# Block heads of a Strassen-Winograd feed-forward kernel: operand sums made from the residual rows through two PSUM banks

## The reference

```python
def rms_norm(x, g):
    xf = x.astype(F32)
    y = xf * lax.rsqrt(jnp.mean(xf * xf, axis=-1, keepdims=True) + EPS)
    return (y * g.astype(F32)).astype(x.dtype)

def swiglu(x, w_in, w_out):
    gate, up = jnp.split(x @ w_in, 2, axis=-1)
    return (jax.nn.silu(gate) * up) @ w_out
...
for l in range(DEPTH):
    x = x + 0.5 * swiglu(rms_norm(x, norm_g[l, 0]), ffn_w_in[l, 0], ffn_w_out[l, 0])
    h = rms_norm(x, norm_g[l, 1])
    ...
    x = x + y
    x = x + 0.5 * swiglu(rms_norm(x, norm_g[l, 2]), ffn_w_in[l, 1], ffn_w_out[l, 1])
```

## Time and profile before

| what | value |
|---|---|
| median of 3 runs | 2114.4 us (2114.19, 2114.4, 2116.44) |
| profiled execution, its own time | 2116.01 us |
| its span, first to last instruction | 2114.2 us |
| TensorE busy | 2052.2 us, 97% |
| VectorE busy | 1257.2 us, 59% |
| ScalarE busy | 872.1 us, 41% |
| GpSimd busy | 1301.0 us, 62% |
| mean granted TensorE clock | 0.991 |
| DMA | 190.61 MB, mean 90 GB/s |

### The profile page before, as it was taken

One profiled execution on the slowest core, in us unless ns is written; L12 is line 12 of the kernel. 1 busy time (PEld: TensorE's weight loads), 2 busy tenths in 40 slices (PEclk: granted clock), 3 DMA queues, 4 the chain that ended last, 5 costly groups with the idle time before them and its releaser, 6 DMA issues.

```text
span 2114.2 us, 41307 instructions
## 1 busy us (share of the span) xinstructions
PE 2052.2 (97%) x16420; PEld 2006.1 (95%) x16420; DVE 1257.2 (59%) x1869; ACT 872.1 (41%) x1643; POOL 1301.0 (62%) x991
## 2 busy tenths in 40 slices
PE   8999999999999899999989999999999999999998
PEld 7999999999989899999989999999998799999997
DVE  7761674424757773476487427744876587725743
ACT  6640661121574560364156226511432445505631
POOL 4774777554415576577657757865633266766774
PEclk9999999999999999999999999999999999999999
DMA  4231232231212232233123312323210232322231
GB/s 137 100 121 67 101 108 101 82 101 62 74 52 81 80 108 82 80 101 123 67 81 101 110 60 100 115 109 109 86 61 31 88 100 81 115 75 95 97 114 48
DMA packets 31702, 190.61 MB, mean 90 GB/s; under 512 B 3888, under 2 KB 6448, under 8 KB 13104
## 3 DMA queue, kind: packets, MB, share of 16 engines
q1 hardware_dynamic: 24192, 173.43, 24.0%
q10 hardware_dynamic: 7344, 14.89, 1.9%
HBM read 180.81 MB, written 7.50 MB: 89 GB/s over the span
## 4 chain that ended last, share of the span: by engine, by line
PE 82%; DVE 7%; ACT 3%; POOL 3%; issue 3%; DMA 2%; ACTq 0%; DVEq 0%; POOLq 0%; SPq 0%
PE ps L591 35%; PE ps L664 31%; PE ps L606 8%; POOL ws L491 2%; DMA wraw<-in_wf_in 2%; POOL sil L510 1%; DVE tg L2303 1%; PE ps L737 1%; DVE tg L2304 1%; PE ps L1417 1%; PE ps L1068 1%; DVE rstd L2106 0%; PE ps L1463 0%; PE ps L764 0%; ACT ws L1677 0%
## 5 line engine op out<-in xcount | busy, mean ns | idle before, releaser
L664 PE MATMUL ps<-tt,ws 128*128 128x272 f32 x3840 | 527.2, 291 | 19.9 <-DVE ws L2248 12.0
L664 PEld LDWEIGHTS ps<-tt,ws 128*128 128x128 f32 x3840 | 501.6, 190 | 23.4 <-DVE ws L2248 13.0
L591 PE MATMUL ps<-a,wh 128*128 128x272 f32 x3028 | 504.4, 289 | 0.0
L554 POOL TENSOR_TENSOR wl<-wraw,wh 128x512 fp32r<-128x512 f32 (+1 forms) x351 | 475.5, 1376 | 13.3
L550 POOL TENSOR_SCALAR wh<-wraw 128x1408 fp32r<-128x1408 f32 (+2 forms) x160 | 180.9, 1130 | 480.2 <-PE ps L591 256.2
L491 POOL TENSOR_TENSOR ws<-wraw,ws 128x512 fp32r<-128x512 f32 x240 | 308.4, 1299 | 237.2 <-ACT ws L1677 114.9
L591 PEld LDWEIGHTS ps<-a,wh 128*128 128x128 f32 x3028 | 427.6, 188 | 1.5 <-POOL wl L554 0.5
L664 PE MATMUL ps<-u,ws 128*128 128x272 f32 x2880 | 402.4, 289 | 12.9 <-DVE snap L2286 10.4
L664 PEld LDWEIGHTS ps<-u,ws 128*128 128x128 f32 x2880 | 377.3, 189 | 14.9 <-issue 12.2
L591 PE MATMUL ps<-a,wl 128*128 128x272 f32 x1514 | 312.7, 287 | 0.0
L2117 DVE SCALAR_TENSOR_TENSOR x<-ps,x 128x544 f32<-128x544 f32 x79 | 57.1, 723 | 354.5 <-PE ps L591 354.5
(11 more groups left out here) (383 smaller groups left out, 2922.0 us busy)
## 6 DMA issues: line engine op xcount, KB each, us to landing
wraw<-in_wf_in SPq DMA_DIRECT2D x87, 1024.0 KB, 4.8
wraw<-in_wf_out SPq DMA_DIRECT2D x32, 1408.0 KB, 6.1
wraw<-in_w_ab SPq DMA_DIRECT2D x12, 1024.0 KB, 4.8
wraw<-in_w_cd SPq DMA_DIRECT2D x10, 1024.0 KB, 4.9
wraw<-in_w_abo SPq DMA_DIRECT2D x8, 512.0 KB, 3.6
wraw<-in_w_cdo SPq DMA_DIRECT2D x8, 512.0 KB, 3.6
wraw<-in_w_bv SPq DMA_DIRECT2D x2, 1024.0 KB, 4.8
out_y<-yout ACTq DMA_DIRECT2D x14, 136.0 KB, 1.9
```

The lines of the kernel that those rows point to most:

```text
L554: piece = nc.gpsimd.tensor_tensor(wl[:, s, some], wraw[:, par_, s * K * P + some.start: s * K * P + some.stop], wh[:, s, some].bitcast(F32 ...
L591: last = nc.tensor.matmul(bank(b0 + 2 * s + half, 0, HT), w[:, s, k * P:(k + 1) * P], act_t[:, k0 + k, part, half * HT:(half + 1) * HT], s ...
L664: last = nc.tensor.matmul(bank(b, 0, HT), ws[weights][w][:, i * P:(i + 1) * P], moving[:, part], start=(start and i == 0 and w == 0 and pa ...
```

## The change

The four sums of a tile are no longer made from a scaled copy of x. ScalarE puts only the corner b12 (the second column half of the tile's first chunk, times gain) into PSUM bank 7 (corner). VectorE makes the four sums from x, with the gain or its negative as a scalar in the same operation, the bank as the second input: E1 into bank 6, E2 over bank 7, T3 and T4 into te (t_sums). ScalarE rounds the E pair out of the two banks and the T pair out of te (t_highs); VectorE writes the low part of E (e_lows), GpSimd that of T (low_t). A tile's corner may enter bank 7 when the low part of the tile before is written. te gets four buffers of half the size, xg goes. The negated gains (less) are made at the start. For the third block (f = 2) tiles 0 to 2 are made during the output products of the second block, behind rows 1, 3 and 5, with tg as the place of T. The head's order on VectorE and ScalarE is written anew. Besides, in all periods: ScalarE takes snapshot 3 of a period (snapshot7) at its end and ahead of glu_high; VectorE makes glu_low after c11 of the next period, and c22 of a half's last period between the two halves of glu. In the opening two uses of PSUM move to other banks.

```diff
+        less = sb("less", [4, TILES7])
...
-        xg = place("xg", [DC, T], F32, a_at + 5 * 8 * T)
-        te = [place(f"te{e}", [4, HT], F32, a_at + 8 * T * (9 + e)) for e in range(2)]
+        te = [place(f"te{e}", [2, HT], F32, a_at + 8 * T * 9 + 8 * HT * e) for e in range(TILES7)]
...
+        def spare(f, i):
+
+            return halves(tg[:, i, :]) if f == 2 and i < 3 else te[i][:]
...
+            def low_t(f, i):
+                pool.wait_ge(t_high, TILES7 * f + i + 1)
+                nc.gpsimd.tensor_tensor(tt[:, i, 2:4, 1, :], spare(f, i), tt[:, i, 2:4, 0, :].bitcast(F32),
+                                        ALU.subtract).then_inc(t3_ready, 1)
...
                 low_a11(seq[0])
+                if g == 0:
+                    low_t(f, 3)
...
+                    if f != 2:
+                        for i in range(3):
+                            low_t(f, i)
...
                         split(i, (first + i) % 2, i // 2, i % 2, SEQ[f][part // 2][-1] if i == 0 else None)
+                        if (f, part) == (1, 3) and i:
+                            low_t(2, i - 1)
...
-                    if p is SEQ[f][0][0] and what in (E1, E2, T4, T3):
+                    if p is SEQ[f][0][0] and what in (E1, E2):
+                        pe.wait_ge(e_low, TILES7 * f + i + 1)
+                    elif p is SEQ[f][0][0] and what in (T4, T3):
...
+                    if n == NORM_OF[2] and m in (1, 3, 5):
+                        corner(2, m // 2)
+                        t_highs(2, m // 2)
...
-                if n:
-                    gained(n, 0, 2)
-                    root(n)
-                    gained(n, 2, 4)
...
+                else:
+                    act.wait_ge(ss_added, (DC - 1) * (n - 1) + DC - 2)
+                    corner(f, 0)
+                    root(n)
+                    t_highs(f, 0)
+                    corner(f, 1)
+                    t_highs(f, 1)
+                    corner(f, 2)
...
+            def corner(f, i):
+
+                t = TILES7 * f + i
+                if t:
+                    act.wait_ge(e_low, t)
+                nc.scalar.activation(bank(B12_BANK, 0, HT), x[:, 2 * i, HT:T], ACT.Identity,
+                                     scale=gamma(f, 2 * i)).then_inc(b12_ready, 1)
+
+            def t_highs(f, i):
+
+                t = TILES7 * f + i
+                act.wait_ge(t_sum, 4 * t + 4)
+                nc.scalar.copy(tt[:, i, 0:2, 0, :], pair(E_BANK)).then_inc(e_high, 1)
+                nc.scalar.copy(tt[:, i, 2:4, 0, :], spare(f, i)).then_inc(t_high, 1)
...
                     if last:
-                        snapshot7(last)
                         high_s2(p, last)
...
-                    if p.end:
-                        snapshot7(p)
-                    if last or before:
-                        glu_high(f, p.i - 1)
                     if next_:
                         high_s1(next_, p)
                         high_a12(next_, p)
+                    snapshot7(p)
+                    if last or before:
+                        glu_high(f, p.i - 1)
...
+                elif f == 2:
+                    t_sums(f, 3)
+                    inv_rms(n)
+                    dve.wait_ge(t3_ready, TILES7 * f + 3)
+                    scaled(0, c0 + 1, tg[:, 0, :])
+                    e_lows(f, 3)
+                    up(0)
                     glu(0)
+                else:
+                    t_sums(f, 0)
+                    inv_rms(n)
+                    scaled(0, c0 + 1, tg[:, 0, :])
+                    e_lows(f, 0)
+                    up(0)
+                    t_sums(f, 1)
+                    e_lows(f, 1)
+                if f != 2:
+                    t_sums(f, 2)
+                    glu(0)
+                    e_lows(f, 2)
+                    t_sums(f, 3)
+                    e_lows(f, 3)
+                scaled(0, c0 + 2, tg[:, 0, :])
+                dve.wait_ge(e_low, TILES7 * (f + 1))
+                sums(p0)
                 glu_low(f, 0)
-                scaled(0, c0 + 2, tg[:, 0, :])
-                t_low_u(f, 3)
+                low1(p0)
                 up(1)
-                sums(p0)
-                lows(p0)
+                low2(p0, True)
                 glu(1)
...
+                dve.wait_ge(b12_ready, t + 1)
+                V.scalar_tensor_tensor(e1, x[:, lo, h1], gamma(f, lo), e2, ALU.mult, ALU.subtract).then_inc(t_sum, 1)
+                V.scalar_tensor_tensor(spare(f, i)[:, T3 - T4, :], x[:, hi, h2], gamma(f, hi), e2, ALU.mult,
+                                       ALU.subtract).then_inc(t_sum, 1)
                 dve.wait_ge(t_sum, 4 * t + 2)
+                V.scalar_tensor_tensor(e2, x[:, hi, h2], minus, e1, ALU.mult, ALU.subtract).then_inc(t_sum, 1)
                 dve.wait_ge(t_sum, 4 * t + 3)
+                V.scalar_tensor_tensor(spare(f, i)[:, 0, :], x[:, hi, h1], minus, e2, ALU.mult,
+                                       ALU.subtract).then_inc(t_sum, 1)
...
+            def e_lows(f, i):
+
+                dve.wait_ge(e_high, TILES7 * f + i + 1)
+                V.tensor_tensor(tt[:, i, 0:2, 1, :], pair(E_BANK), tt[:, i, 0:2, 0, :].bitcast(F32),
+                                ALU.subtract).then_inc(e_low, 1)
...
                         c11(last)
+                        if n > 1 or g == 0:
+                            glu_low(f, last.i - 1)
...
-                        glu(last)
+                        glu(last, p if p.end else None)
```

118 lines of the change are left out of this document (49 added, 69 removed).

## The result

The changed kernel takes **2078.5 us** (median of 4 runs, 2075.54 to 2080.2), the kernel before in runs beside it 2114.3 us (4 runs, 2113.94 to 2116.44). The ratio is 0.9827, with a 95% interval of 0.9814 to 0.9839. That is 35.8 us less. The forecast was 43.4 us less, 2071 us, with a range of 2059 to 2087.

A forecast was written before the change was run, and what follows sets the result against it. TensorE was taken as the bound, nearly always busy, idling in heads, seams and period gaps. Heads 24.6, periods 9.2 and seams 9.6 give 43.4 us less: 2072.6, or 2071 us against the median of runs; 8 in 10 within 2059 to 2087.

The forecast's parts named there:

- likeliest case: Whole kernel: the forecast's own case, a time between 2066 and 2076 us, chance 0.57.
- head of block 1: First block's head: P5 at 38.85 and first P2 at 41.85 instead of 50.57, gain 8.7 us.
- head of block 2: Second block's head: P5 starts at 703.6 and not at 708.51, gain 4.9 us.
- head of block 3: Third block's head: only tile 3 left there, TensorE's own stream the bound, no stop, gain 7.8 us.
- head of block 4: Fourth block's head: P5 3.9 us earlier, less 0.7 for slower clock, gain 3.2 us.
- period gaps: Inside periods: TensorE's 11 waits for snapshot 3 go, with restarts, gain 9.2 us.
- seams: Ends of the eight half blocks: earlier c22 starts the last product 1.43 us sooner; 1.2 us counted each, gain 9.6 us.
- seams give back what they gain: Rival at seams: VectorE holds behind GpSimd delay the output product's last row; gain about 0, 2081 us, chance 0.13.
- a tile step: Heads: corner, four sums, rounding and low part through two banks take 3.6 us a tile; over 4 us means wrong.
- the slow 4.64: Second block's head: the 24 matmuls of P5 and P6 stay at 4.64 us, where 3.0 would do.
- Four tiny negations run before x arrives: Opening, listed under side costs: the four small negations come before x is there; no time was counted for them.
- T's low parts on VectorE: Heads: alternative to GpSimd for the T pair's low parts; judged to add 2.6 us to VectorE's chain.

The follow-up runs named there:

- orders_only: Kernel before with only the new order of periods and seams, heads as before: 2111.3 us, ratio 0.9976 to the kernel before.
- seam_undone: Changed kernel with its seams alone put back to the old order (glu_low ahead of c22, c22 behind both halves of glu): 2079.4 us, ratio 0.9826.
- seam_high_act: Changed kernel with the rounding of the first 1408 columns of the first output weights moved from GpSimd to ScalarE at seams: 2070.2 us, ratio 0.9781.
- best: Changed kernel plus seam rounding on ScalarE, a shorter chain ahead of P5 with A12 earlier, and negated gains made later: 2067.0 us, ratio 0.9772.
- block3_in_head: Changed kernel without the third block's special case, all four tiles made in its head: 2081.5 us, ratio 0.9838.
- head_short2: Changed kernel with VectorE and ScalarE reordered in heads of blocks 1, 2, 4 for a shorter chain ahead of P5, A12 rounded earlier: 2076.3 us, ratio 0.9823.

## Why the prediction was off by 7.5 us

The range and the sign held; the likeliest case did not. The spans are 38.5 us apart, which splits like this:

| term | forecast | measured in the traces |
|---|---|---|
| head of block 1 | 8.7 | 6.8 |
| head of block 2 | 4.9 | 6.0 |
| head of block 3 | 7.8 | 7.9 |
| head of block 4 | 3.2 | 3.5 |
| period gaps | 9.2 | 9.5 (7.9 and 11 restarts) |
| seams | 9.6 | -0.9 (36.8 before, 37.8 after, by starts as in orders_only) |
| place of the weights | not seen | 4.6 |
| rest, not assigned | | 1.1 |

**Luck.** The range held with the help of two things that the forecast didn't have. The faster pace of the outputs came from where the new tile happened to push the weights; at the old place the same program takes 2085.5 us, 1.5 us inside the upper end. And P5 and P6 of the second head ran at full clock in this trace, which they do in some executions only.

**Seams: the step that failed** is "I take 1.2 us a seam, 8 seams". It asked of each seam what is late for the last product of the half and for the output product's last row, and not what the output product needs first, its weights. The rival "seams give back what they gain" had the size (2081 us) and the wrong mechanism: the last row was never late. The row that decides was in the trace of before: GpSimd's L554 ended 0.06 us ahead of the product that uses it. c22 did come early and the last product did follow directly, as forecast; TensorE then stood 1.4 to 1.5 us at each seam for the output weights. seam_undone and orders_only show the term at about zero or a little below, and seam_high_act shows whose the wait is.

**Heads.** Right in sum, 24.2 against 24.6. P5 of block 2 came 18.7 us behind the reciprocal's end (675.14 to 693.85), forecast 18.3; a tile step is 3.97 and not 3.6 us (over 4 was the forecast's sign of being wrong), the sums 0.50 us each and not 0.44, the corner 0.49 and not 0.39. For the sums the forecast had the right row, L2959 with 493 ns, and set it aside. Block 2's own gain was larger than forecast, because P5 and P6 came at full clock (3.09 us) where I had kept the slow 4.64. Block 1's was smaller. "Four tiny negations run before x arrives" was wrong: x was there, and the four took 2.18 us, so the low part of u began at 7.96 and not at 6.70 and the second pair started 1.3 us later, not 0.14. In best, where they are moved away, it is still 0.8 us later than before, so they are not the whole of it.

**Clock.** The forecast took slow matmuls behind the second head's stop for given. They come in some executions and not in others. Windows of 4 us behind P5's start, in the changed kernel and then in seam_undone, whose head has the same instructions:

```profile
694.00:698.00 4.00, 4.00 (x33) 4.00 (x34) 3.76 (x5) 1.90 (x5) 4.00 (x4) 1.00 0.01 4
```

```profile
694.00:698.00 4.00, 4.00 (x21) 4.00 (x20) 2.71 (x4) 0.00 (x1) 3.20 (x3) 0.53 0.02 4
```

33 matmuls at a granted clock of 1.00, 21 at 0.53. Three of the five traces with this head (seam_undone, seam_high_act, block3_in_head) had it, at about 2.2 us each. The same two stops stand in block 4's head of all five and in block 3's of block3_in_head, and there no trace lost more than 0.4 us. A second place of this kind lies in the first mixer: in the window of 578 to 592 us the changed kernel's trace has 101 matmuls at a granted clock of 0.76, head_short2's 117 at 1.00, and that stretch (from the first block's end to the second head's sum of squares) is 2.8 us longer in the former. The changed kernel's runs scatter over 4.7 us, and their mean clocks (0.995 to 0.998) go with their times. So a difference of 2 us between two such kernels can't be read from four runs.

**Third block.** No stop in its head, as forecast. In the rows of the outputs where the tiles are made the spacing stays at 8.2 us (evacuations at 989.56 and 997.77).

**The sums from x** read x, a scalar from a tile and PSUM: do they wait for GpSimd? In the second head they took 0.49 to 0.51 us while GpSimd ran its two low parts of T (L498, 679.83 to 682.52). By the Trainium skill, GPSIMD Engine Reference, section 8 (Key points), contention is with instructions of two SBUF inputs (or in a 2-port mode); the trace agrees, and a scalar from SBUF does not count as one of them here. The other choice weighed in the forecast, T's low parts on VectorE, was not run.

## What to carry to other kernels

When a wait of 1 us is about to go, look at everything that the next instructions need, and at how long each of it had been ready: what ended within that microsecond of the old start takes the wait over. The matmul's bracket doesn't show it in the old trace; here the small bracket of its weight load did. A gain made at the front of a pipeline is kept only if all that feeds the next stages comes earlier as well. And when a new tile moves others, compare the pace of an undisturbed stretch in both traces first, or its difference is taken for the change's own.

## What was unexpected of the hardware

**The place of tiles in SBUF changes the pace of fp32r matmuls of 272 columns.** With wh 32 bytes behind a multiple of 128, 528 output matmuls took 65.81 to 65.84 us, with 0, 64 or 96 bytes 66.39 to 66.41 us: 124.7 and 125.8 ns each, in every trace of this case, at a granted clock of 1.00. The period products, whose weights moved by the same bytes, took 1.50 to 1.51 us for 12 at both. Which of the moved tiles it is stays open.

**TensorE's granted clock after the same stops differs between executions**: 1.00 in two traces and 0.53 to 0.65 in three, in the window of 694 to 698 us behind stops of 2.4 and 1.0 to 1.4 us.

**Tiny instructions of VectorE on SBUF can be held behind GpSimd.** The four negations (4 elements a partition, each waiting for the one before) took 2.18 us together, but not evenly. The first two took 0.22 and 0.17 us. The third ran from 6.21 to 7.34 and the fourth from 7.38 to 7.93; GpSimd's L551 and L565 ended at 7.31 and 7.90 beside them:

```profile
6.03 1.28 POOL L551 TENSOR_TENSOR wl<-wraw,wh 128x512 fp32r<-128x512 f32 x1
```

In best, three of the same instructions, with no GpSimd instruction beside them, took 0.57 us together (at 388.99). That GpSimd is the cause is read from these ends and wasn't tried by itself.
